# Thirty-two instead of sixteen tokens of a mixed block by gathered rows, and the gate step's differences on ScalarE

## The reference, cut to what matters

```
def peer_ffn(h, wq, sub_keys, expert_u, expert_v):
    def block(xb):                                  # 128 tokens
        q = (xb @ wq).reshape(128, 8, 2, 128)
        s = einsum('thpd,hpkd->thpk', q, sub_keys)
        s_top, i_top = top_k(s, 16)
        cand_s = s_top[:, :, 0, :, None] + s_top[:, :, 1, None, :]   # 16 x 16 pairs
        cand_i = i_top[:, :, 0, :, None] * 128 + i_top[:, :, 1, None, :]
        best_s, best_pos = top_k(cand_s, 16)
        experts = take_along_axis(cand_i, best_pos)
        g = softmax(best_s)
        act = gelu(einsum('thkd,td->thk', expert_u[experts], xb))
        return einsum('thk,thkd->td', g * act, expert_v[experts])
```

## Time and profile before

| | |
|---|---|
| median of 3 runs | 2411.23 us (2410.53 to 2413.74) |
| the profiled execution's span | 2411.4 us |
| TensorE busy / weight load busy | 98% / 88% |
| VectorE, ScalarE, GpSimd busy | 65%, 39%, 52% |
| mean rate of the transfers | 218 GB/s; 396 GB/s from 1087 to 1600 us |
| granted TensorE clock | 0.998 |

### The profile page before, as it was taken

One profiled execution on the slowest core, in us unless ns is written; L12 is line 12 of the kernel. 1 busy time (PEld: TensorE's weight loads), 2 busy tenths in 40 slices (PEclk: granted clock), 3 DMA queues, 4 the chain that ended last, 5 costly groups with the idle time before them and its releaser, 6 DMA issues.

```text
span 2411.4 us, 35928 instructions
## 1 busy us (share of the span) xinstructions
PE 2367.4 (98%) x12892; PEld 2127.2 (88%) x12892; DVE 1567.8 (65%) x2831; ACT 945.5 (39%) x1488; POOL 1244.2 (52%) x704
## 2 busy tenths in 40 slices
PE   7999999999999999999999999999999999999998
PEld 4878887899999999999999999997777888888886
DVE  5258535689899999779999999892266225422201
ACT  4374333344455555333333333342353223332312
POOL 2305443337899999555555555444304444444443
PEclk9999999999999999999999999999999999999999
DMA  7227522327978898999999999943202222222231
GB/s 283 80 115 258 182 91 84 133 94 255 324 252 301 299 328 309 396 379 414 416 415 409 417 408 414 370 166 106 82 14 96 97 96 96 96 93 99 90 102 70
DMA packets 179613, 526.14 MB, mean 218 GB/s; under 512 B 18240, under 2 KB 70896, under 8 KB 178224
## 3 DMA queue, kind: packets, MB, share of 16 engines
q1 hardware_dynamic: 120928, 345.24, 39.7%
q0 software_dynamic: 43024, 159.14, 17.0%
q10 hardware_dynamic: 15552, 20.36, 2.4%
HBM read 474.93 MB, written 49.73 MB: 218 GB/s over the span
## 4 chain that ended last, share of the span: by engine, by line
PE 91%; DVE 3%; DMA 2%; issue 2%; POOL 1%; ACT 1%; SPq 0%; ACTq 0%; DVEq 0%; POOLq 0%
PE bank L1372 21%; PE bank L1374 21%; PE bank L1373 21%; PE pair L1373 6%; PE pair L1372 6%; PE pair L1374 6%; PE pair L1726 1%; POOL wlo L714 1%; DMA wraw<-in_w 1%; PE bank L1889 1%; PE pair L1513 1%; PE bank L1552 1%; PE bank L1539 1%; DMA act_dram<-actb 1%; PE pair L1664 1%
## 5 line engine op out<-in xcount | busy, mean ns | idle before, releaser
L714 POOL TENSOR_TENSOR wlo<-wraw,whi 128x1024 fp32r<-128x1024 f32 x303 | 740.4, 2446 | 761.1 <-ACT whi L856 760.2
L1372 PE MATMUL bank<-HH,whi 128*128 128x512 f32 (+1 forms) x2048 | 740.2, 361 | 9.5 <-DMA T<-in_keys 3.0
L1373 PE MATMUL bank<-HL,whi 128*128 128x512 f32 (+1 forms) x2048 | 735.8, 359 | 0.0
L1374 PE MATMUL bank<-HH,wlo 128*128 128x512 f32 (+1 forms) x2048 | 735.7, 359 | 0.0
L856 ACT ACTIVATE whi<-wraw 128x1024 fp32r<-128x1024 f32 x456 | 481.8, 1058 | 632.2 <-PE pair L1374 337.4
L1372 PEld LDWEIGHTS bank<-HH,whi 128*128 128x128 f32 x2048 | 385.0, 188 | 54.8 <-issue 5.7
L1374 PEld LDWEIGHTS bank<-HH,wlo 128*128 128x128 f32 x2048 | 384.5, 188 | 40.3
L1373 PEld LDWEIGHTS bank<-HL,whi 128*128 128x128 f32 x2048 | 385.0, 188 | 39.6 <-issue 0.5
L780 POOL DMA_INDIRECT VROW<-in_w,which x128 | 206.0, 1609 | 190.5 <-DVE YROW L2522 178.0
L2454 DVE TENSOR_TENSOR wlo<-wraw,whi 128x1024 fp32r<-128x1024 f32 x153 | 186.4, 1219 | 20.9 <-ACT whi L856 20.0
L773 POOL DMA_INDIRECT X<-in_u_rows,which x128 | 149.0, 1164 | 57.3 <-DVE dots L2296 32.6
(11 more groups left out here) (447 smaller groups left out, 3815.1 us busy)
## 6 DMA issues: line engine op xcount, KB each, us to landing
wraw<-in_w SPq DMA_DIRECT2D x456, 512.0 KB
gate_dram<-GS SPq DMA_DIRECT2D x24, 1024.0 KB
GJ<-gate_dram SPq DMA_DIRECT2D x32, 768.0 KB
act_dram<-actb ACTq DMA_DIRECT2D x108, 184.0 KB
AJ<-act_dram SPq DMA_DIRECT2D x108, 184.0 KB
adaw<-in_ada SPq DMA_DIRECT2D x32, 512.0 KB
ada<-in_ada SPq DMA_DIRECT2D x16, 512.0 KB, 14.2
NB<-in_nab POOLq DMA_DIRECT2D x4, 1024.0 KB
```

The lines of the kernel that those rows point to most:

```text
L714: nc.gpsimd.tensor_tensor(wlo[:, slot, :, :].rearrange("p k c -> p (k c)"), wraw[:, slot, :, :].rearrange("p k c -> p (k c)"), whi[:, slot ...
L1372: pe.matmul(out_, ah, bh, start=first, stop=False, **kw)
L1373: pe.matmul(out_, ah, bl, start=False, stop=False, **kw)
L1374: return pe.matmul(out_, al, bh, start=False, stop=last, **kw)
```

## The change

`FT` becomes 32, so SD = 352, STEPS = 88, FS = 4 and DOTS = 160: the dense matmuls have 352 columns, and there are 32 gathers of each kind for the third block's last 32 tokens. The differences `OJ` move from GpSimd (one instruction of 128x512 a step) to ScalarE (four activations of 128x128 with a scale of -1 and a bias from `JTS`), at the head of its iteration, three steps ahead. The dots are spread anew: 28 in the lead, 58 in the gate stage, 66 in the tail, 8 in the V stage. In the tail GpSimd also does the `lo` of tiles 103 to 114, with its gathers between them, and VectorE those from 115 on.

```diff
-FT = 16
+FT = 32
-U_POOL = 4 * GATE_IT + GATE_TILES + 3
+U_TAIL = 4 * GATE_IT + GATE_TILES + 3
+U_POOL = 115
-GATE_DOT = 2
-PSUM_DOTS = TOP_DOTS + STEPS // GATE_DOT
-U_DOTS = 112
+GATE_DOTS = 58
+PSUM_DOTS = TOP_DOTS + GATE_DOTS
+TAIL_DOTS = 66
+U_DOTS = PSUM_DOTS + TAIL_DOTS
-V_DOT_TILES = [10 * m // 3 + 1 for m in range(32)][:DOTS - U_DOTS]
+V_DOT_TILES = [12 * m + 1 for m in range(DOTS - U_DOTS)]
...
+        def gate_dots(q):
+            return GATE_DOTS * q // STEPS
...
@@ gpsimd
-            def offsets_j(q):
-                if q >= 4:
-                    pool.wait_ge(og_ready, q - 3)
-                nc.gpsimd.tensor_tensor(OJ[:, q % 4, :, :], bc(iota[:, :], 1, 4), bc(JTS[:, q * 4:q * 4 + 4], 2, P),
-                                        ALU.subtract).then_inc(oj_ready, 1)
-            pool.wait_ge(j_rows, 1)
             for q in range(STEPS):
-                offsets_j(q)
                 if (lows - gate0 - 3) * STEPS // GATE_TILES + 1 == q:
                     lo(G0["U"] + lows, lows % R)
                     lows += 1
-                if q >= 2 * GATE_DOT and q % GATE_DOT == 0:
+                while fetched < R + TOP_DOTS + gate_dots(max(q - 2, 0)):
                     fetch_u(fetched)
                     fetched += 1
             for t in range(lows, U_POOL):
                 lo(G0["U"] + t, t % R)
-            for k in range(fetched, U_DOTS + R):
+                while fetched < R + PSUM_DOTS + (t - U_TAIL + 1) * TAIL_DOTS // (P - U_TAIL):
+                    fetch_u(fetched)
+                    fetched += 1
+            u_fetches = min(U_DOTS + R, DOTS)
+            for k in range(fetched, u_fetches):
                 fetch_u(k)
...
@@ scalar
+            def offsets_j(q):
+                if q >= 4:
+                    act.wait_ge(og_ready, q - 3)
+                for t in range(4):
+                    ins = nc.scalar.activation(OJ[:, q % 4, t, :], iota[:, :], ACT.Identity, scale=-1.0,
+                                               bias=JTS[:, 4 * q + t:4 * q + t + 1])
+                ins.then_inc(oj_ready, 1)
             ahead(G0["U"], 4 * GATE_IT)
+            act.wait_ge(j_rows, 1)
+            for q in range(3):
+                offsets_j(q)
             for n in range(STEPS + 2):
+                if n + 3 < STEPS:
+                    offsets_j(n + 3)
                 for h in range(2 * n - 4, 2 * n - 2):
...
@@ vector
                 gates_hot(q)
-                if q % GATE_DOT == GATE_DOT - 1:
+                while dotted[0] < TOP_DOTS + gate_dots(q + 1):
                     dot()
...
-            v.wait_ge(w_lo, G0["U"] + U_POOL)
-            tail_dots = U_DOTS - PSUM_DOTS
-            for t in range(U_POOL, P):
-                lo(G0["U"] + t, t % R)
-                while dotted[0] < PSUM_DOTS + (t - U_POOL + 1) * tail_dots // (P - U_POOL):
+            for t in range(U_TAIL, P):
+                if t == U_POOL:
+                    v.wait_ge(w_lo, G0["U"] + U_POOL)
+                if t >= U_POOL:
+                    lo(G0["U"] + t, t % R)
+                while dotted[0] < PSUM_DOTS + (t - U_TAIL + 1) * TAIL_DOTS // (P - U_TAIL):
                     dot()
```

More of the change, by code:

```diff
@@ L820, in _ @@
                 pool.wait_ge(g_out[b], 64 * TD)
-            fetched = U_DOTS + R
+            fetched = u_fetches
             for n, k in enumerate(V_ROWS):
```

## The result

The changed kernel takes 2484.9 us (median of 4 runs, 2484.0 to 2486.0) against 2411.3 us beside it (2410.5 to 2413.7): ratio 1.0302, 95% interval 1.0287 to 1.0317. It is slower by 73.6 us; the prediction had 42.7 and a range that ended at 2482. The profiled execution has a span of 2484.2 us against 2411.4, so the two traces can be laid side by side. (It took 2486.0 us: 1.8 us lie outside the span.

The account below looks back on a forecast made before the run. It took TensorE, VectorE and GpSimd to be at their limit together in the gate stage, and TensorE and transfers in the tail and V stage; 2411.4 + 22 (gate) + 31 (tail) - 10 (V) = 2454 us, range 2415 to 2482.

Parts of the forecast that it names:

- The loop through ScalarE: Gate stage: highs queue behind activations waiting for the previous step's `gates_hot`, a 3.36 us loop limiting steps without a dot.
- The bytes of the tail: Tail: 66 dots instead of 38 bring 14.7 MB more by gathers, 59.7 MB in all.
- ScalarE's sum: Gate stage: ScalarE's own load, 3.54 us in the two steps of three that have a tile.
- Rival (1): Tail and V stage: transfers are not the limit; tail 111 us, V stage 492, kernel 2410; chance 0.12.
- (2): Gate stage: ScalarE's loop does not close, VectorE bounds, stage ends at 971 us, kernel 2429; chance 0.12.
- (3): Gate stage: an activation costs 0.36 to 0.4 us or tables change; 42 to 60 us more, kernel 2505; chance 0.08.
- The tail, +65 instead of +31: Last `gates_hot` to first `V` tile: 146 us instead of 115.2, bytes at about 404 GB/s, so 31 us more.
- Only four are ahead: Tail: each dot needs a gather of 128 rows of 4 KB, and only four gathers are issued ahead.
- GpSimd's 135 us: Tail: GpSimd's work of 12 low differences and 66 gathers at 1.3 + 0.3 us, called near the limit.
- The gate stage, +30 instead of +22: First to last `gates_hot`: 58 steps of 3.56 us and 30 of 3.42, 309 us in all, 22 us more.
- The lead, -4.7 instead of +1.4: Lead: no gain, TensorE comes 6.2 us earlier and waits; first `gates_hot` at 687.4 us against 686.0.
- The V stage, -21 instead of -10: V stage: 96 tiles at 3.94 us, held by transfers at 417 GB/s, then 32 at 3.84; 501 us against 511.

Follow-up runs that it names:

- t3: The changed kernel with ScalarE's two gate_high put ahead of the four activations of the differences, no work added: 2454.7 us, ratio 1.0171.
- t4: The kernel before with only the differences moved to ScalarE, in the place the change gives them: 2456.2 us, ratio 1.0177.
- t8: The kernel before with only the differences moved to ScalarE, but queued behind the high parts: 2414.2 us, ratio 1.0007.
- t1: The changed kernel with all low differences of tiles 103 to 127 on VectorE, GpSimd only gathering in the tail: 2472.1 us, ratio 1.0242.
- t10: As t1, but the tail's 66 dots take 64 of 1024 columns while gathers still bring whole rows: 2459.3 us, ratio 1.0200.
- t11: As t1, but the gathers of the tail's 66 dots bring 128 rows of 2 KB instead of 4 KB: 2455.6 us, ratio 1.0179.
- t5: The changed kernel with all the tail's dots reading their token row from PSUM: 2470.0 us, ratio 1.0236.
- t7: The changed kernel with t1 and t3 combined and dots split 28 + 58 + 56 (tail) + 18 (V stage): 2443.2 us, ratio 1.0123.
- t6: The changed kernel with t1 and t3 combined and dots split 28 + 70 (gate steps) + 44 (tail) + 18 (V stage): 2439.5 us, ratio 1.0103.

## Why the prediction was wrong

**Right.** The loop through ScalarE, its members and its waits: t3, t4 and t8 show that queue order alone makes it. The bytes of the tail, within 3%. What did not bound: TensorE in the gate stage, and ScalarE's sum. Rival (1) is excluded by its tail of 111 us, though its V stage (492 us, at TensorE's own pace) came nearer than the forecast's; (2) by a gate stage that ended at 1000 us and not 971; (3) by 0.29 us an activation.

**The tail, +65 instead of +31: the step that failed.** "The most that a stretch of this mix carried ... is 404 GB/s: 148 and 145 us. I take 146." That turns bytes into time by a rate, and takes for granted that the requests stand ready. "Only four are ahead" stood a few sentences before, and was not priced; GpSimd's 135 us were set beside the 146 as a smaller sum, where they stand in line with the gathers. With t1's latency under load of 8 us, a dot and an issue, a round of four is 9.5 us; the kernel before, with 38 dots in its tail, would need 9.5 rounds or 90 us of its 115 and doesn't notice; with 66 it needs 157. t1 has 167.7: fourteen such rounds on its chain, and some 25 us of low differences, further dots and gathers' instructions between them. t10, where only the dots are shorter, shows that in t1 it is the round and not the rate; t11 shows that halving a gather's bytes takes 1.3 of 8.0 us off its latency on the chain, and that GpSimd's issue stands close behind. How the rest of the latency divides between sharing the engines with 512 KB loads and a floor was not tested.

Of the 34 us that were missing, 6 are size (61.3 MB at 404 GB/s are 152 us, not 146), some 15 the ring (t1 against t10, which has those bytes at that rate), and 12 to 13 are those of t1 and t5.

**These 13 us of the tail** had no term at all: VectorE and GpSimd stopping each other. The sign was in the earlier trace rows, where a gather's instruction takes 0.95 us in the gate stage and 1.87 in the tail. The prediction took 0.95 as its lower bound of GpSimd's cost and a mean of 1.33 in its sum, without asking what made them differ. The change moved low differences of GpSimd (tiles 103 to 114) in among dots that read two SBUF operands; before, none of them met. t5, which changes only where a dot reads, gives the price.

**The gate stage, +30 instead of +22: a term mis-sized.** 0.29 us an activation for 0.24, taken from the earlier trace rows, where the instruction behind is another kind (a read of the accumulator). Four of them add 0.2 us to a loop that was put at 3.36, 3.57 in all against 3.62 measured; that covers the steps with dots (3.56), so all 88 steps go at its pace. The Trainium skill, "ScalarE: Activation LUTs", section "Rules for kernel authors", gave 0.41 us; the trace has 0.39 for the duration of one (mean of 328) and 0.29 from start to start, so the rule fits a duration but not the pace of a row of them.

**The lead, -4.7 instead of +1.4.** "TensorE would come 6.2 us earlier and wait: VectorE's 28 dots and the search are unchanged." The work is unchanged, its waits were not: 7.1 us of waiting for gathers that GpSimd issues at TensorE's pace. 679.40 and 679.47 us in the earlier trace rows looked like VectorE holding TensorE up; both hung on the same tiles.

**The V stage, -21 instead of -10.** The forecast let TensorE run at 3.94 us a tile while transfers carry 417 GB/s. They did carry 416 in the fourth row of the table of stretches after, but TensorE was busy 120 of 120 us at 3.84, and waits for 1 us in the whole stage: the 21 us are all of its columns (128 x 24 x 6.6 ns = 20), what rival (1) gave the stage. In the 369 us of the first 96 tiles the transfers moved 153.0 MB, 415 GB/s, where the forecast counted 96 x 1.644 = 157.8. Issued in them are 94 loads of `V`, 94 of `AJ`, 125 gathers of `V` rows and 4 of `U` rows, where the forecast counted 96, 96, 128 and 8: four `U` gathers had been issued before the stage, and the lead of the others shrank by two or three items. So buffers that are full at the start made up for a deficit of 3% over 96 tiles. With ten dots more TensorE waits 17 us for `WL`, and each costs 2.2 us (t7); that the reserve is then gone early is the likely reason, not a measured one.

## What to carry to other kernels

Where a transfer goes through a ring of n buffers, price it as rounds: (latency under load + use + issue) / n for each, beside bytes over rate, and take the larger as a lower bound. With 8.0 us and 404 GB/s that gives 157, 139, 123 and 152 us for the tails of t1, t7, t6 and t10, which measured 168, 150, 128 and 153: other work in the same queues comes on top, up to 11 us here and more where GpSimd also had low differences (180). The cheap test is to shorten the use of the data and leave the bytes alone. When instructions are added to an in-order queue, ask first which instruction behind them another engine is waiting for: the same four activations cost 42 us or nothing by their place. And when one instruction has two durations in a trace, find what differs before using either.

## What the runs showed of the hardware

- A VectorE dot with both operands in SBUF waits for a whole `tensor_tensor` of GpSimd: 1.22 us becomes up to 4.08, and each of the eight that were stopped in the changed kernel's tail ends 1.09 us behind the low difference. With one operand in PSUM there is no such stop (1.220 us on the mean of 67).
- The issue of a gather on GpSimd takes 0.93 to 0.95 us by itself or during a VectorE dot that reads PSUM (18 in t5), and up to 1.99 where it begins during a VectorE instruction with both operands in SBUF.
- A gather of 64 rows of 4 KB, to partitions 0 to 63, kept the DMA engines as busy (0.97) as one of 128 rows; 128 rows of 2 KB took their share to 0.76 to 0.85 in the three later stretches of t11's tail. The share of busy time says nothing of how many bytes more would fit.
- TensorE's granted clock was 1.00 in the first 19 us of the changed kernel's tail, with TensorE busy for 18.5 of 18.8, and 0.72 to 0.91 in the eight stretches of 20 us behind, with TensorE busy for 11.5 to 17.3 of each 20. On the chain it costs little: in t10 twenty matmuls at the tail's end, under 3 us. There a 352-column matmul stands at the 1.2 GHz level and then at 2.4:

```profile
1148.97 0.29 PE bank L1388
...
1154.52 0.17 PE bank L1389
1154.68 0.16 PE bank L1387
```
